# Value products of the prompt attention, moved into the interruption that follows them in the matmul stream

## What is computed

```
s = einsum(q, k) * ATTN_SCALE, masked to a window of 128
m = maximum(max(s), sink)
p = exp(s - m)
p = p / (sum(p) + exp(sink - m))
out = einsum(p, v)
```

## The kernel before, in words

| slot | TensorE | ScalarE | VectorE |
|---|---|---|---|
| 2 | score 1, turn 0 | turned 0, queries | scores 1 |
| 3 | values 0 | exps 1, out_hi 0 | probs 1, out_lo 0 |
| 4 | score 2, turn 1 | turned 1 | scores 2 |
| 5 | values 1 | exps 2, out_hi 1 | probs 2, out_lo 1 |
| 6 | score 3, turn 2 | turned 2 | scores 3 |
| 7 | values 2 | exps 3, out_hi 2 | probs 3, out_lo 2 |
| 8 | turn 3 | turned 3 | (none) |
| 9 | values 3, sample scores | out_hi 3 | out_lo 3 |

## Time and profile before

### The profile page before, as it was taken

How to read it: one execution, slowest core, us unless ns; L and a number is a source line. 1 busy time by engine, 2 the same in 40 slices (tenths; PEclk the granted TensorE clock), 3 DMA queues, 4 the chain that set the end, 5 groups by cost and what they waited for, 6 DMA issues and landing times.

```text
span 2561.3 us, 51163 instructions
## 1 busy us (share of the span) xinstructions
PE 2537.4 (99%) x19380; PEld 2507.1 (98%) x19380; DVE 1464.5 (57%) x2010; ACT 1016.6 (40%) x1412; POOL 331.4 (13%) x279
## 2 busy tenths in 40 slices
PE   8999999999999999999999999999999999999998
PEld 8999999999999999999999999999999999999998
DVE  6578787555554355555545777775555443555544
ACT  5354554333333333333334545443333333333333
POOL 2011003111110011111100110131111000111111
PEclk9999999999999999999999999999999999999999
DMA  6445445444445444544455554445444455444443
GB/s 224 161 160 181 159 144 169 162 169 159 168 158 170 164 164 158 169 161 167 164 163 167 170 178 152 135 159 175 163 164 163 165 162 165 164 164 163 165 164 136
DMA packets 116510, 420.75 MB, mean 164 GB/s; under 512 B 13840, under 2 KB 15120, under 8 KB 116368
## 3 DMA queue, kind: packets, MB, share of 16 engines
q1 hardware_dynamic: 109296, 397.72, 46.3%
q0 software_dynamic: 4112, 14.78, 1.8%
q10 hardware_dynamic: 3024, 7.16, 0.9%
HBM read 411.06 MB, written 11.87 MB: 165 GB/s over the span
## 4 chain that ended last, share of the span: by engine, by line
PE 98%; DVE 1%; ACT 0%; POOL 0%; DMA 0%; issue 0%; DVEq 0%; SPq 0%; ACTq 0%; POOLq 0%
PE gp L1573 32%; PE gp L1575 31%; PE gp L1574 31%; PE mb L1629 1%; PE mb L1740 1%; PE mb L1761 1%; PE mb L1753 0%; POOL acc L1500 0%; DVE rstd L788 0%; DMA raw<-wstream 0%; PE mb L1638 0%; PE mb L1687 0%; ACT xh L661 0%; PE mb L1704 0%; DVE wlo L763 0%
## 5 line engine op out<-in xcount | busy, mean ns | idle before, releaser
L1573 PE MATMUL gp<-xh,whi 128*128 128x288 f32 x4096 | 1224.8, 299 | 12.4 <-DVE xl L1249 9.7
L1574 PE MATMUL gp<-xl,whi 128*128 128x288 f32 x4096 | 1209.2, 295 | 0.0
L1575 PE MATMUL gp<-xh,wlo 128*128 128x288 f32 x4096 | 1205.4, 294 | 0.0
L763 DVE TENSOR_TENSOR wlo<-raw,whi 128x1024 fp32r<-128x1024 f32 x754 | 972.6, 1323 | 354.8 <-ACT whi L424 351.2
L424 ACT ACTIVATE whi<-raw 128x1024 fp32r<-128x1024 f32 x754 | 768.7, 1052 | 578.6 <-PE gp L1575 553.4
L1573 PEld LDWEIGHTS gp<-xh,whi 128*128 128x128 f32 x4096 | 768.6, 188 | 21.1 <-issue 20.0
L1575 PEld LDWEIGHTS gp<-xh,wlo 128*128 128x128 f32 x4096 | 772.1, 189 | 0.0
L1574 PEld LDWEIGHTS gp<-xl,whi 128*128 128x128 f32 x4096 | 770.0, 188 | 0.6
L1573 PE MATMUL gp<-fh,whi 128*128 128x288 f32 x1408 | 416.7, 296 | 0.0
L1574 PE MATMUL gp<-fl,whi 128*128 128x288 f32 x1408 | 415.4, 295 | 0.0
L1575 PE MATMUL gp<-fh,wlo 128*128 128x288 f32 x1408 | 414.0, 294 | 0.0
(11 more groups left out here) (264 smaller groups left out, 1770.4 us busy)
## 6 DMA issues: line engine op xcount, KB each, us to landing
raw<-wstream SPq DMA_DIRECT2D x754, 512.0 KB, 4.2
s<-s_cache POOLq DMA_DIRECT2D x8, 512.0 KB, 10.7
hs_out<-s ACTq DMA_DIRECT2D x8, 512.0 KB, 3.3
caches_out<-caches POOLq DMA_DIRECT2D x8, 496.0 KB, 8.7
x<-x_in ACTq DMA_DIRECT2D x4, 576.0 KB, 8.8
kct<-kt_cache POOLq DMA_DIRECT2D x4, 512.0 KB, 5.2
vct<-v_cache POOLq DMA_DIRECT2D x4, 512.0 KB, 6.7
y_out<-x SPq DMA_DIRECT2D x3, 576.0 KB, 2.9
```

The lines of the kernel that those rows point to most:

```text
L763: v.tensor_tensor(wlo[slot][:], raw[slot][:], whi[slot][:].bitcast(F32), ALU.subtract).then_inc(lo_ready, 1)
L1573: t.matmul(out, w_hi, mv_hi, start=first, stop=False)
L1574: t.matmul(out, w_hi, mv_lo, start=False, stop=False)
L1575: mm = t.matmul(out, w_lo, mv_hi, start=False, stop=end)
```

## The change

`values(u-1)` moves from a slot of its own to the head of the next unit's interruption, ahead of `score(u+1)` and `turn(u)`, and `values(2)` moves ahead of `turn(3)`; the slots they leave stay empty. To let the probabilities of the next unit stand beside the values of the last, the six transposes fill all of `mb[2]` and columns 0 to 255 of `mb[3]`, and the values go to columns 256 to 511 of `mb[3]`. `turned` copies 512 and 256 columns in place of twice 384. `turn(u)` waits for `pT{u-1}` in place of `al{u-1}`, and `values(u)` waits for `al{u-1}` too. On ScalarE `out_hi(u-1)` follows `turned(u)`; on VectorE `out_lo(u-1)` follows `probs(u+1)`, but `out_lo(2)` stands in slot 9, right ahead of `out_lo(3)`. The slots after:

| slot | TensorE | ScalarE | VectorE |
|---|---|---|---|
| 2 | score 1, turn 0 | turned 0, queries | scores 1 |
| 3 | (none) | exps 1 | probs 1 |
| 4 | values 0, score 2, turn 1 | turned 1, out_hi 0 | scores 2 |
| 5 | (none) | exps 2 | probs 2, out_lo 0 |
| 6 | values 1, score 3, turn 2 | turned 2, out_hi 1 | scores 3 |
| 7 | (none) | exps 3 | probs 3, out_lo 1 |
| 8 | values 2, turn 3 | turned 3, out_hi 2 | (none) |
| 9 | values 3, sample scores | out_hi 3 | out_lo 2, out_lo 3 |

The diff, without the lists of step names, which follow the new order:

```diff
 def turned(u):
     a.wait_ge(at.sem, at.at(T, f"pt{u}"))
-    for i in range(2):
-        m = a.activation(pT[u % 2][:, i, :], mb[2 + i][:, 0:3 * P], ACT.Copy)
-    m.then_inc(aa.sem, aa.step(f"pT{u}"))
+    flat = pT[u % 2][:].rearrange("p i c -> p (i c)")
+    a.activation(flat[:, 0:4 * P], mb[2][:], ACT.Copy)
+    a.activation(flat[:, 4 * P:], mb[3][:, 0:2 * P], ACT.Copy).then_inc(aa.sem, aa.step(f"pT{u}"))
...
 def out_hi(u):
     a.wait_ge(at.sem, at.at(T, f"pv{u}"))
-    a.activation(out[:, 4 + u, 0:SEQ], mb[2][:, 0:SEQ], ACT.Copy).then_inc(aa.sem, aa.step(f"ah{u}"))
+    a.activation(out[:, 4 + u, 0:SEQ], mb[3][:, 2 * P:], ACT.Copy).then_inc(aa.sem, aa.step(f"ah{u}"))
...
     turned(u)
     if u == 0:
         queries()
+    else:
+        out_hi(u - 1)
     yield
     exps(u + 1)
-    out_hi(u)
     yield
 turned(3)
+out_hi(2)
 yield
 out_hi(3)
...
 def out_lo(u):
     v.wait_ge(aa.sem, aa.at(T, f"ah{u}"))
-    v.tensor_tensor(out_l[:, 4 + u, 0:SEQ], mb[2][:, 0:SEQ], out[:, 4 + u, 0:SEQ].bitcast(F32), ALU.subtract
+    v.tensor_tensor(out_l[:, 4 + u, 0:SEQ], mb[3][:, 2 * P:], out[:, 4 + u, 0:SEQ].bitcast(F32), ALU.subtract
                     ).then_inc(av.sem, av.step(f"al{u}"))
...
 probs(1)
+yield
+scores(2)
+yield
+probs(2)
 out_lo(0)
 yield
-scores(2)
-yield
-probs(2)
+scores(3)
+yield
+probs(3)
 out_lo(1)
 yield
-scores(3)
-yield
-probs(3)
+yield
 out_lo(2)
-yield
-yield
 out_lo(3)
...
 def turn(u):
-    if u:
-        t.wait_ge(av.sem, av.at(T, f"al{u - 1}"))
-    else:
-        t.wait_ge(aa.sem, aa.at(T, "kvt"))
+    t.wait_ge(aa.sem, aa.at(T, f"pT{u - 1}" if u else "kvt"))
     t.wait_ge(av.sem, av.at(T, f"p{u}"))
     for i in range(2):
         for c in range(3):
-            mm = t.transpose(mb[2 + i][:, c * P:(c + 1) * P], sc[u % 2][:, i, c * P:(c + 1) * P], ident)
+            k = 3 * i + c
+            mm = t.transpose(mb[2 + k // 4][:, k % 4 * P:(k % 4 + 1) * P], sc[u % 2][:, i, c * P:(c + 1) * P],
+                             ident)
     mm.then_inc(at.sem, at.step(f"pt{u}"))
 
 def values(u):
     t.wait_ge(aa.sem, aa.at(T, f"pT{u}"))
+    if u:
+        t.wait_ge(av.sem, av.at(T, f"al{u - 1}"))
     for m_ in range(2):
         for i in range(2):
...
-            mm = t.matmul(mb[2][rows, m_ * P:SEQ], kvt[:, m_, kv], pT[u % 2][:, i, 2 * m_ * P:(2 + m_) * P],
+            mm = t.matmul(mb[3][rows, (2 + m_) * P:], kvt[:, m_, kv], pT[u % 2][:, i, 2 * m_ * P:(2 + m_) * P],
                           start=(m_ == 0), stop=(m_ == 1))
     mm.then_inc(at.sem, at.step(f"pv{u}"))
...
 for u in range(3):
+    if u:
+        values(u - 1)
     score(u + 1)
     turn(u)
     yield
-    values(u)
     yield
+values(2)
 turn(3)
 yield
 values(3)
```

More of the change, by code:

```diff
@@ L340, in build @@
         av = Steps(sem("attn_vector"), ["sc0", "mx0", "mm0", "nm0", "ds0", "den0", "rec0", "p0"]
[3 rows of a table removed]
[3 rows of a table added]
                    + ["ssn", "smx", "smm", "snm", "sds", "sden", "srec", "sp", "asb", "sal"])
-        aa = Steps(sem("attn_scalar"), ["krx", "es0", "kvt", "pT0", "qs", "es1", "ah0", "pT1", "es2", "ah1", "pT2", "es3", "ah2",
-                                        "pT3", "ah3", "ses", "pts", "sah"])
+        aa = Steps(sem("attn_scalar"), ["krx", "es0", "kvt", "pT0", "qs", "es1", "pT1", "ah0", "es2", "pT2", "ah1", "es3", "pT3", "ah2",
+                                        "ah3", "ses", "pts", "sah"])
         ap_ = Steps(sem("attn_gpsimd"), ["qs0", "stored"])
@@ L1134, in attn @@
                 probs(1)
-                out_lo(0)
                 yield
@@ L1139, in attn @@
                 probs(2)
-                out_lo(1)
+                out_lo(0)
                 yield
@@ L1144, in attn @@
                 probs(3)
-                out_lo(2)
+                out_lo(1)
                 yield
                 yield
+                out_lo(2)
                 out_lo(3)
```

## The result

The changed kernel takes 2567.77 us (median of 20 runs, 2567.4 to 2568.18), beside 2563.87 us for 20 runs of the kernel before on the same chip: a ratio of 1.0016 [1.001, 1.0022], 3.9 us longer. On a second chip, the changed kernel took 2566.79 us beside 2562.80, 4.0 us longer. The forecast was 3.2 us longer.

A forecast was written before the change was run, and what follows sets the result against it. TensorE was taken as the bound, its matmuls busy 2537.4 of 2561.3 us. Waits less savings gave +0.44 and +1.18 us for the two kinds of call, twice 1.62, +3.2: 2566.8 us, own range 2565.0 to 2568.4.

The forecast's parts named there:

- The merging: On TensorE, joined interruptions save 0.19 us twice and 0.05 once per call: 0.43 us a call, 1.7 for four.
- The step from values into scores: On TensorE, 64-column outputs into 64-row operands, not seen before: taken as 0.80 us, ends about 0.17 less or more.
- estimate by the count of such changes: By the skill's drain rule, merging saves eight drains on TensorE, some 0.8 us for the way in alone.
- The places of the waits: values waits for out_lo ten times: slot 9 of every call, slots 6 and 8 of second and fourth, slot 6 otherwise.
- first kind of call: The first call and its repeat in layer 1: waits 0.24 and 0.63 us, less 0.43 saved, +0.44 us each.
- VectorE's queue bounds the second kind of call: VectorE also carries conv: 9.38 us between out_lo two slots apart, TensorE needs 8.84; that call +1.18 us.
- The size of the waits: TensorE waiting for out_lo: 0.24 and 0.63 us (slots 6, 9) in first call; 0.64, 0.54, 0.63 (6, 8, 9) in second.
- 0.05 us from end to start: From out_lo's end on VectorE to TensorE's next start: 0.05 us, read at transposes and used for values.
- the waits are covered: Rival: out_lo is there in time everywhere, so TensorE gains the 1.7 and 0.4 us: 2561.5 us, chance 0.08.
- ScalarE holds the queue up: Rival: out_hi ahead of exps delays every out_lo by 0.26 us, twelve times, 3.1 us more: 2569.9 us, chance 0.08.
- The clock falls: Rival: TensorE's clock drops behind a wait, 2.0 us a fall; one in each call gives 2575.0 us, chance 0.03.
- The merging saves nothing: Rival: values into scores costs as much as a return to the stream, 0.19 lost where unswallowed: 2567.5 us, no separate chance.

The follow-up runs named there:

- the waits swapped: Changed kernel with values(u) waiting for out_lo's step (al{u-1}) first and turned's (pT{u}) second: 2566.17 us beside 2562.84 for the kernel before, ratio 1.0012.

## Why the prediction was right

**The merging**, 0.43 us for each call: right. The step from values into scores, taken as 0.80 between ends of 0.17 to either side, is 0.81; the interruption is 2.73 us long, and undoing the merging gives 0.42 us back in a call.

The Trainium skill, TensorEngine Tiling (Array Packing), Key Properties, says that changing the tiling mode drains TensorE. The prediction's estimate by the count of such changes was 0.8 us for the whole; the traces give 1.7. That TensorE drains at such a change isn't refuted, but the count of the changes was not the price here, since the second matmul behind an interruption, 0.21 to 0.24 us against 0.133, is paid once less too.

**The places of the waits**: right, all ten, and the one slot without a wait (slot 8 of the first kind of call) as well, with 0.54 us of cover where 0.4 was forecast. The forecast that VectorE's queue bounds the second kind of call held: `out_lo` to `out_lo` is 346.54 to 355.94, 9.40 us beside the 9.38 of the earlier trace rows.

**The size of the waits**: the term that was mis-sized. The step "0.05 us from end to start" was read at the transposes, which had one semaphore to wait for, and applied to `values`, which has two. It measured 0.14. Eight of the ten restarts lengthen a call by the 0.09 us, 0.7 in all, and 3.2 + 0.7 = 3.9, beside 4.1 and 3.9 by the calls of the two traces. Place by place `values` comes later by 0.35 and 0.76 us in slot 6 (forecast 0.24 and 0.64), by 0.54 in slot 8 (0.54) and by 0.75 in slot 9 (0.63). Slot 8 shows no excess, and shows 0.54 with the waits swapped as well: VectorE's queue sets the distance from the wait before it, and both restart alike. What is left beyond the restart is at most 0.03 us a place and not the same in both profiles of the kernel. With the waits swapped the calls measured +0.44 and +1.16, beside the +0.44 and +1.18 on record.

**The rivals**: *the waits are covered* fell by the view of who waited, though it became the faster kernel once VectorE's order was changed. *ScalarE holds the queue up* fell: the calls of the swapped kernel leave no room for 0.26 us at each wait. *The clock falls* did not happen (granted clock 0.999, and no steps of 0.24 us in the calls), but its mechanism is real: waits of 2.37 and 3.69 us brought it about, and no row here shows it at 1.97 us or less. *The merging saves nothing* fell.

## What to carry to other kernels

When work is moved to the head of an interruption on the engine that bounds the kernel, its waits move with it: price the saving of the merge and the arrival of every awaited result separately, and move the producers as well. Here the change alone lost 3.9 us, and the same change with three `out_lo` placed earlier in a queue that had room gained 2.2 to 2.4. Where one instruction waits for two semaphores, try writing the one that comes last first, and look at the gap from the producer's end to the consumer's start: here it was worth 0.09 us at each wait.

## What the runs showed of the hardware

- TensorE restarts 0.04 to 0.06 us after the awaited VectorE instruction ends when the weight load carries that wait, at all three shapes seen (scores, transposes, values) and behind waits of 0.1 to 3.7 us, and 0.14 to 0.15 us after it when the wait is an instruction of its own ahead of the weight load.
- Behind waits of 2.37 and 3.69 us in the middle of full work TensorE ran at 0.24 us a step for a while (granted clock 0.50 to 0.52), which cost 1.5 to 2.7 us each; behind 1.97 us and the 0.1 to 0.8 us of the other waits it did not.
